# Where the high and low parts of split operands begin within their tiles

## The reference

```
layer 0 mixer: proj = norm(h) @ w_in
               Re 2-D DFT of 4 groups of 256 channels  |  GLU -> depthwise conv of 31 taps -> LayerNorm -> SiLU
               h += concat(both) @ w_out
layer 1 mixer: B, C, x = split(norm(h) @ w_in);  h += (B * conv3(C * x)) @ w_out
every layer:   h += square(relu(norm(h) @ w1)) @ w2          (w1: 2048 x 8192)
```

## Time and profile before

| | before |
|---|---|
| median of three runs | 2116.27 us |
| the profiled execution | 2116.13 us |
| its span, first to last instruction | 2114.1 us |
| TensorE busy | 2089.6 us (99%) |
| VectorE busy | 1281.1 us (61%) |
| ScalarE busy | 927.1 us (44%) |
| mean granted TensorE clock | 0.998 of full |
| DMA engines' mean busy share | about half, 181 GB/s of reads |

### The profile page before, as it was taken

One profiled execution on the slowest core, in us unless ns is written; L12 is line 12 of the kernel. 1 busy time (PEld: TensorE's weight loads), 2 busy tenths in 40 slices (PEclk: granted clock), 3 DMA queues, 4 the chain that ended last, 5 costly groups with the idle time before them and its releaser, 6 DMA issues.

```text
span 2114.1 us, 36370 instructions
## 1 busy us (share of the span) xinstructions
PE 2089.6 (99%) x15226; PEld 1985.3 (94%) x15226; DVE 1281.1 (61%) x1300; ACT 927.1 (44%) x965; POOL 66.1 (3%) x40
## 2 busy tenths in 40 slices
PE   8999999999999999999999999999999999999997
PEld 8999999999999999999999999888888888888886
DVE  8999975545554554556566556665556555555555
ACT  6434464334434443445433334545335434434443
POOL 1001020000000000000100000010000000000001
PEclk9999999999999999999999999999999999999999
DMA  7442455555555555554555455455554554554552
GB/s 283 178 160 101 162 185 192 179 181 187 188 180 179 183 189 183 179 180 177 196 183 179 179 189 189 168 202 187 187 191 179 198 181 178 197 188 178 193 195 80
DMA packets 55336, 383.91 MB, mean 182 GB/s; under 512 B 6176, under 2 KB 8224, under 8 KB 9312
## 3 DMA queue, kind: packets, MB, share of 16 engines
q1 hardware_dynamic: 54880, 381.84, 50.1%
q0 software_dynamic: 240, 1.02, 0.1%
q10 hardware_dynamic: 144, 0.04, 0.0%
HBM read 380.78 MB, written 2.10 MB: 181 GB/s over the span
## 4 chain that ended last, share of the span: by engine, by line
PE 96%; DVE 2%; ACT 1%; issue 0%; DMA 0%; DVEq 0%; SPq 0%
PE banks L310 25%; PE banks L304 20%; PE banks L302 19%; PE banks L303 19%; PE banks L311 13%; DVE wl L796 1%; ACT wh L519 0%; DVE h L824 0%; ACT xs L536 0%; DMA raw<-weights 0%; DVE ssum L935 0%; DVE h L1149 0%; DVE h L1155 0%; ACT sq L546 0%; PE banks L437 0%
## 5 line engine op out<-in xcount | busy, mean ns | idle before, releaser
L796 DVE TENSOR_TENSOR wl<-raw,wh 128x1024 fp32r<-128x1024 f32 x720 | 891.9, 1249 | 720.6 <-ACT wh L519 719.5
L519 ACT ACTIVATE wh<-raw 128x1024 fp32r<-128x1024 f32 x720 | 753.9, 1058 | 971.3 <-PE banks L304 610.9
L302 PE MATMUL banks<-xs,wh 128*128 128x258 f32 (+1 forms) x2176 | 618.3, 284 | 10.3 <-DVE wl L796 10.3
L304 PE MATMUL banks<-xs,wl 128*128 128x258 f32 (+1 forms) x2176 | 621.1, 285 | 0.0
L303 PE MATMUL banks<-xs,wh 128*128 128x258 f32 (+1 forms) x2176 | 614.3, 282 | 0.0
L310 PE MATMUL banks<-hid,wh 128*128 128x512 f32 x1280 | 448.5, 395 | 0.0
L302 PEld LDWEIGHTS banks<-xs,wh 128*128 128x128 f32 x2176 | 412.4, 190 | 10.6 <-issue 8.8
L303 PEld LDWEIGHTS banks<-xs,wh 128*128 128x128 f32 x2176 | 411.4, 189 | 0.1
L304 PEld LDWEIGHTS banks<-xs,wl 128*128 128x128 f32 x2176 | 409.9, 188 | 0.0
L304 PE MATMUL banks<-hid,wl 128*128 128x258 f32 x1280 | 363.8, 284 | 0.0
L302 PE MATMUL banks<-hid,wh 128*128 128x258 f32 x1280 | 361.9, 283 | 1.4 <-DVE hid L840 1.4
(11 more groups left out here) (103 smaller groups left out, 779.5 us busy)
## 6 DMA issues: line engine op xcount, KB each, us to landing
raw<-weights SPq DMA_DIRECT2D x359, 1024.0 KB, 4.8
out<-h SPq DMA_DIRECT2D x8, 256.0 KB, 2.7
h<-x SPq DMA_DIRECT2D x3, 544.0 KB, 10.6
raw<-weights SPq DMA_DIRECT2D x2, 512.0 KB, 6.0
conv<-dft_seq POOLq DMA_DIRECT2D x1, 580.5 KB, 13.2
h<-x SPq DMA_DIRECT2D x2, 272.0 KB, 4.3
act<-dft_ch POOLq DMA_DIRECT2D x1, 258.0 KB, 7.9
par<-params POOLq DMA_DIRECT2D x1, 160.0 KB, 6.4
```

What stands on the lines that cost most here:

```text
L302: pe.matmul(dst, w[0], v[0], start=start, stop=False)
L304: return pe.matmul(dst, w[1], v[0], start=False, stop=stop)
L519: act.activation(wh[:, j % RING, :, :], src.rearrange("p (t c) -> p t c", t=SLAB_K), ACT.Copy).then_inc(high_ready, 1)
L796: dve.tensor_tensor(wl[:, j % RING, :, :], src.rearrange("p (t c) -> p t c", t=SLAB_K), wh[:, j % RING, :, :].bitcast(F32), ALU.subtract). ...
```

## The change

`high_of` returns columns 0 to L - lo of the tile instead of lo to L. `low_of_tile` returns the columns from L - lo on where the two parts fit into 512 columns together (lo = 16), and from L on otherwise. `both_of`, used for lo = 16 only, returns both, from column 0. All callers stay as they are.

```diff
--- before.py
+++ after.py
@@ -172,14 +172,16 @@
 
 
 
+
         def high_of(t, tile, lo):
-            return t[:, tile, lo:L]
+            return t[:, tile, 0:L - lo]
 
         def low_of_tile(t, tile, lo):
-            return t[:, tile, L:2 * L - lo]
+            at = L - lo if 2 * (L - lo) <= COLS else L
+            return t[:, tile, at:at + L - lo]
 
         def both_of(t, tile, lo):
-            return t[:, tile, lo:2 * L - lo]
+            return t[:, tile, 0:2 * (L - lo)]
 
         def quad(g):
             return slice(M * g, M * g + M)
```

## The result

The changed kernel takes 2123.38 us (median of 7 runs, 2122.95 to 2124.34) against 2115.98 us (7 runs): ratio 1.0036, 95% interval 1.0025 to 1.0047. I had forecast 2115.8 in a range that ended at 2120.

A forecast was written before the change was run, and what follows sets the result against it. TensorE, busy 2089.6 of 2114.1 us, was taken as the bound, through its matmul pitch. Lead-in 14 gave -0.5 us and the other terms 0: 2116.13 - 0.5 = 2115.6, or 2115.8 on the median's scale, range 2107 to 2120.

The forecast's parts named there:

- TensorE's pitch decides, and the rest doesn't: Whole kernel: a change counts if it alters the time from one matmul's start to the next, and little elsewhere.
- The term for lead-in 14: 258-column products: moving the high part from byte 56 to 0 wins at most about 0.05 ns a matmul; taken as -0.5 us.
- The term for lead-in 16: 512- and 256-column pairs: both starts stay multiples of 64 bytes, so cost 0.
- the same line: Pitch as 0.442 ns a column plus 5.4 ns, from two aligned stages; 119.4 ns at 258 columns against 119.5 measured.
- The count of cachelines: 258-column high reads: 65 lines of 16 bytes from byte 56 and from byte 0, so nothing to win.
- L303's shorter duration as the price of the others' misalignment: Layer 0's MLP: 280 ns against 282 and 284 would return 6 ns a product, 18.4 us; gain above 0.2% given chance 0.17.
- Rival 2: Last 820 us: start modulo 128 sets the 512-wide read, byte 0 bad; 3 ns a pair, 2123.2 us; chance 0.08.
- The engines that write and reread: ScalarE and VectorE on the high and low parts: nothing gained or lost within 3 ns an instruction, 0.2 us, hidden.

The follow-up runs named there:

- run 1: Only the four lead-in 14 stages got the new starts (14, 272 to 0, 272), on the kernel before: 2127.30 us against 2116.23, ratio 1.0054.
- run 2: Only the three lead-in 16 stages got the new starts (16, 272 to 0, 256), on the kernel before: 2112.36 us, ratio 0.9982.
- run 3: The kernel before with new starts in all seven stages at once, such as 14, 286 and 8, 280: 2122.89 us (one run).

## Why the prediction was wrong

- *TensorE's pitch decides, and the rest doesn't.* Right: the whole difference lies in the pitch of two kinds of stage, with clock, waits and chain as before.
- *The term for lead-in 14: "At 258 columns that gives 119.4 ns ... The misalignment therefore leaves at most about 0.05 ns a matmul to win."* This is the step that failed. It took the pitch for a function of the number of columns, so that two aligned stages would give an aligned 258-column matmul. Measured, such a matmul takes 120.7 ns (2897.8 / 24), and other starts give 118.9 (0, 286) to 122.2 (8, 280 in its slow pattern) at the same 258 columns. The +-1.5 us that I allowed came from counting (9216 matmuls at the 0.2 ns named there are 1.8 us), not from the assumption. I named that at the end as what could be wrong, but only for a gain, and gave it no width. In place of the -0.5 us of this term the runs show +11.9 us by slabs and +11.1 us timed (run 1).
- *The term for lead-in 16, cost 0.* Wrong: -3.8 us (run 2). I saw that the start modulo 128 changes and priced it at 3 ns either way; the size measured, 1.67 ns a pair, is within that. I dismissed it by the same line. The 3 ns came from L310's mean duration, which did fall from 395 to 392; but L311's rose from 280 to 281, and a duration isn't a pitch.
- *The count of cachelines.* The Trainium skill's "SBUF — State Buffer", section "Specifications (TRN2)", prices a read by the 16-byte lines it crosses; 65 before and 65 after would leave the 258-column stages as they were. Run 1 has them at 3.9 ns a product more, so the number of lines does not decide here.
- *L303's shorter duration as the price of the others' misalignment.* Not believed, rightly: with all starts aligned nothing fell to 280, and L303's own unmoved read got longer.
- *Rival 2* named 2123.2, and the result is 2123.4. That is a coincidence. Its place was the last 820 us, and these got faster; the loss is in the first 1290.
- *The engines that write and reread.* Right: no trace of a cost, as far as the spans and counts can show.
- *The range.* Both unknowns were bounded on the gain's side (18.4 us) and on the loss's only by 6.9 in one kind of stage. The loss in the lead-in 14 stages, 11.9 us, had no bound at all above 1.5, though a pattern that can fall by 6 ns a product can rise by 4.

What stays open is the mechanism below the rule. The runs show that the time of a product depends on where its moving reads start relative to the weight reads and to each other, and that a stage may settle in one of several steady patterns. That the two reads contend for parts of the on-chip memory would fit, but I did not find a formula that gives the times in the table, and no run separates such contention from, say, an arbiter inside TensorE.

## What to carry to other kernels

An alignment is not good or bad by itself for a TensorE-bound stream: rounder starts cost 1.1% in one stage and gave 0.5% in another, and the best starts found (column 0 with 286, and column 31) follow no rule that one would write down. In a stage of this kernel without waits the time of a slab repeats to a nanosecond, or does so in a cycle of three slabs, so one can give every stage its own starts and read seven candidates from one profile. Then time the winner as a whole, because a stage's pattern can change with the starts of other stages and after an interruption. And treat the address of the weight tiles as a parameter: moving a small tile in front of them changed the slab times of all three kinds of stage here.

## What the runs showed of the hardware that I had not expected

- The steady time of a slab goes in steps. Of the settled times, 2773.3, 2786.7, 2800.0, 2813.3, 2826.7, 2840.0, 2853.3, 2866.7, 2880.0, 2893.3, 2906.7, 2933.3, 3000.0 and 3013.3 ns lie on one ladder of 13.33 ns, 1.67 ns a product, which is 4 periods of the 2.4 GHz at which the granted clock of 1.00 runs TensorE. 2809, 2860, 2871, 2897.8 and 2995.5 lie between its rungs. All of these but 2860 come with slabs that differ among themselves in a cycle of three (2895, 2896, 2902 in run 1), and over its three slabs such a cycle is on the ladder too: 8693.3 ns are 652 steps.
- The same instructions on the same addresses ran at 2880.0 or 2933.3 ns a slab, 1.8% apart, quarter by quarter (run 3). A few matmuls on other operands or one hold-up can move a running stage from one such time to another (2853.3 to 2866.7 and 2880 to 2906.7 in run 3).
- The three lines of a product show different mean durations that are no prices of their operands: moving the high part changed the means of all three lines and of two weight loads.
- Between the slowest and the fastest start seen lie 3.8% at lead-in 16 (2880.0 and 2773.3) and 2.8% at lead-in 14 (2933.3 and 2853.3).
